# State reads of a retention layer: two batches at a time, on two 32-column strips of the array

## The reference, cut to what matters

```python
def retention_chunk(state, q, k, v, log_g):
    ...
    scores = jnp.einsum('bthd,bshd->bhts', q, k) * decay[None]
    inner = jnp.einsum('bhts,bshe->bthe', scores, v)
    q_decay = jnp.exp((i[:, None] + 1.0) * log_g[None, :])
    cross = jnp.einsum('bthd,bhde->bthe', q * q_decay[None, :, :, None], state)
    k_decay = jnp.exp((t - 1.0 - i)[:, None] * log_g[None, :])
    new_state = jnp.exp(t * log_g)[None, :, None, None] * state + jnp.einsum('bshd,bshe->bhde', k * k_decay[None, :, :, None], v)
    return new_state, inner + cross
```

## Time and profile before

| | |
|---|---|
| median of 3 runs | 3668.87 us (3668.02 to 3674.22) |
| span of the profiled execution | 3665.9 us |
| TensorE (PE) matmul busy, share of the span | 94% |
| VectorE (DVE), ScalarE (ACT), GpSimd (POOL) busy | 29%, 26%, 29% |
| DMA, mean over the span | 104 GB/s |
| mean granted TensorE clock | 0.977 of full |

### The profile page before, as it was taken

How to read it: one execution, slowest core, us unless ns; L and a number is a source line. 1 busy time by engine, 2 the same in 40 slices (tenths; PEclk the granted TensorE clock), 3 DMA queues, 4 the chain that set the end, 5 groups by cost and what they waited for, 6 DMA issues and landing times.

```text
span 3665.9 us, 43692 instructions
## 1 busy us (share of the span) xinstructions
PE 3442.4 (94%) x15505; PEld 2678.1 (73%) x15505; DVE 1048.2 (29%) x1920; ACT 947.2 (26%) x1465; POOL 1066.0 (29%) x444
## 2 busy tenths in 40 slices
PE   6799999999989889999999999999999989999877
PEld 5687777777877677686867767686867768778766
DVE  3401243232222341404132231404132240212234
ACT  4422333233223232121212212121212221222232
POOL 5542222232332023232322223232322223333211
PEclk9899999999999899999999999999999999999988
DMA  7333221223222233333333333333333444422231
GB/s 248 99 100 88 71 64 57 65 66 121 80 81 86 87 107 103 111 118 115 118 109 100 115 109 108 112 118 112 118 109 106 128 134 153 132 75 80 75 103 69
DMA packets 211747, 380.60 MB, mean 104 GB/s; under 512 B 20448, under 2 KB 59232, under 8 KB 207520
## 3 DMA queue, kind: packets, MB, share of 16 engines
q1 hardware_dynamic: 137744, 233.34, 20.6%
q10 hardware_dynamic: 73824, 144.84, 11.9%
HBM read 318.95 MB, written 60.16 MB: 103 GB/s over the span
## 4 chain that ended last, share of the span: by engine, by line
PE 72%; DVE 8%; issue 1%; ACT 1%; DVEq 1%; ACTq 0%
PE bank L544 17%; PE bank L546 16%; PE bank L545 16%; PE bank L548 4%; PE bank L549 4%; PE bank L855 2%; DVE R L1763 2%; PE bank L560 2%; PE bank L864 2%; PE bank L579 2%; DVE R L1761 1%; PE bank L903 1%; PE bank L899 1%; PE bank L825 1%; DVE stat L1501 1%
## 5 line engine op out<-in xcount | busy, mean ns | idle before, releaser
L521 POOL TENSOR_TENSOR w_lo<-w_raw,w_hi 128x1024 fp32r<-128x1024 f32 x440 | 1065.7, 2424 | 2554.8 <-ACT w_hi L961 2554.3
L544 PE MATMUL bank<-w_hi,xT_hi 128*128 128x512 f32 (+1 forms) x2880 | 1164.9, 404 | 20.5 <-DVE xT_sample L1526 8.9
L546 PE MATMUL bank<-w_hi,xT_lo 128*128 128x512 f32 (+1 forms) x2880 | 1123.4, 390 | 0.0
L545 PE MATMUL bank<-w_lo,xT_hi 128*128 128x512 f32 (+1 forms) x2880 | 1123.1, 390 | 0.0
L961 ACT ACTIVATE w_hi<-w_raw 128x1024 fp32r<-128x1024 f32 x440 | 466.2, 1061 | 1784.9 <-PE bank L549 1641.8
L544 PEld LDWEIGHTS bank<-w_hi,xT_hi 128*128 128x128 f32 x2880 | 545.5, 189 | 160.2 <-issue 29.8
L545 PEld LDWEIGHTS bank<-w_lo,xT_hi 128*128 128x128 f32 x2880 | 546.0, 190 | 115.8 <-issue 11.5
L546 PEld LDWEIGHTS bank<-w_hi,xT_lo 128*128 128x128 f32 x2880 | 544.8, 189 | 114.8
L548 PE MATMUL bank<-w_hi,xT_sample 128*128 128x512 f32 (+1 forms) x816 | 328.0, 402 | 5.2 <-DVE R L1761 5.2
L549 PE MATMUL bank<-w_lo,xT_sample 128*128 128x512 f32 (+1 forms) x816 | 316.8, 389 | 0.0
L973 ACT ACTIVATE R<-bank 128x512 f32<-128x512 f32 (+5 forms) x304 | 158.4, 526 | 371.1 <-PE bank L560 266.7
(11 more groups left out here) (171 smaller groups left out, 2485.6 us busy)
## 6 DMA issues: line engine op xcount, KB each, us to landing
w_raw<-in_w_in_ret SPq DMA_DIRECT2D x128, 512.0 KB, 3.7
w_raw<-in_w_in_even SPq DMA_DIRECT2D x80, 512.0 KB, 3.6
w_raw<-in_w_in_ret SPq DMA_DIRECT2D x128, 256.0 KB, 2.9
R<-in_state_ret ACTq DMA_DIRECT2D x64, 512.0 KB, 4.7
out_ret_state_sample<-R ACTq DMA_DIRECT2D x64, 512.0 KB, 3.1
w_raw<-in_w_out_ret SPq DMA_DIRECT2D x64, 512.0 KB, 3.6
w_raw<-in_w_out_even SPq DMA_DIRECT2D x32, 512.0 KB, 3.6
mix_scratch<-R ACTq DMA_DIRECT2D x16, 576.0 KB, 3.8
```

Source lines behind the costliest of these rows:

```text
L521: pool.tensor_tensor(wlo[:, s], raw[:, s], whi[:, s].bitcast(F32), ALU.subtract).then_inc(lo_ready, 1)
L544: pe.matmul(acc, th[:, k, tok], hi[:, kk, 0:width], start=first, stop=False)
L545: pe.matmul(acc, th[:, k, tok], lo[:, kk, 0:width], start=False, stop=False)
L546: mm = pe.matmul(acc, tl[:, k, tok], hi[:, kk, 0:width], start=False, stop=last)
```

## The change

The state reads of two batches are issued together. The batches are taken in the order `ORD` = 0, 4, 1, 5, 2, 6, 3, 7, for loads, stores, masked keys and reads alike. At even steps b the pair (b, b + 1) of that order is read: one of the batches 0 to 3, whose rows are 0 to 31 of the output, and one of the batches 4 to 7, whose rows are 32 to 63. `qz` holds 32 columns per batch in place of 64. Both states of a pair are waited for, each wait on an instruction of its own; then for each k there are two matmuls with a stationary operand of 128 x 32, one writing partitions 0 to 31 of bank 5, the other 32 to 63. At odd steps there is no state read; the state updates stay where they were.

```diff
+ORD = [b for g in range(DEC_B // 2) for b in (g, g + DEC_B // 2)]
+HB = NS // 2
...
-        qz, zm, rdec = c.take(2, DEC_B, NS), c.take(DEC_B, NS), c.take(P + NS)
+        qz, zm, rdec = c.take(2, DEC_B, HB), c.take(DEC_B, NS), c.take(P + NS)
...
-                    if m == 0:
-
-                        pe.wait_ge(state_in[b % 4], 32 * h + (16 * (b // 4) + 16))
+                    if m == 0 and b % 2 == 0:
+
+                        for n in (b, b + 1):
+                            pe.wait_ge(state_in[n % 4], 32 * h + (16 * (n // 4) + 16))
+                            wait_apart()
                         for k in range(2):
-                            mm = pe.matmul(bank[5][0:NS, :], qz[:, k, b], Wst[:, b % 4, k], start=False, stop=(b == 7 and k == 1))
-                        if b == 7:
+                            for n in (b, b + 1):
+                                half = slice(HB * (ORD[n] // 4), HB * (ORD[n] // 4) + HB)
+                                mm = pe.matmul(bank[5][half, :], qz[:, k, ORD[n]], Wst[:, n % 4, k], start=False, stop=(b == 6 and k == 1))
+                        if b == 6:
                             mm.then_inc(FULL(stage, "OI"), 1)
...
-                src = I.state_ret[0].rearrange("b h (k p) e -> b h p k e", p=P)[b, h]
+                src = I.state_ret[0].rearrange("b h (k p) e -> b h p k e", p=P)[ORD[b], h]
...
-                    dst = O.ret_state_sample[0].rearrange("b h (k p) e -> b h p k e", p=P)[b, h]
+                    dst = O.ret_state_sample[0].rearrange("b h (k p) e -> b h p k e", p=P)[ORD[b], h]
...
                     for k in range(2):
-                        ins = v.tensor_tensor(qz[:, k], qkT[:, k, SEQ:SEQ + NS].unsqueeze(1).to_broadcast([P, DEC_B, NS]), zm, ALU.mult)
+                        for g in range(2):
+                            q = qkT[:, k, SEQ + HB * g:SEQ + HB * (g + 1)].unsqueeze(1).to_broadcast([P, DEC_B // 2, HB])
+                            ins = v.tensor_tensor(qz[:, k, 4 * g:4 * g + 4], q, zm[:, 0:4, 0:HB], ALU.mult)
...
-                keys, col = QK[:, NT, RK:2 * RK], kz[:, bass.ds(DEC_B * h + b, 1)]
+                keys, col = QK[:, NT, RK:2 * RK], kz[:, bass.ds(DEC_B * h + ORD[b], 1)]
```

## The result

The changed kernel takes 3685.7 us (median of five runs, 3684.8 to 3687.3); the kernel before, beside it, 3670.9 (3668.0 to 3675.7). The ratio is 1.0042 [1.0029, 1.0055]: slower by some 15 us. The forecast was 3684.3. The state reads keep PE busy for 62 us less and the kernel is slower all the same.

The account below looks back on a forecast made before the run. PE was taken to bound the kernel, with 72% of the chain. The span of 3665.9 us, less 10.2 won, plus 25.6 for the clock, gave 3681.3; 3.0 up to the median made 3684.3, range 3659 to 3698 (8 in 10).

Parts of the forecast that it names:

- Even steps, 0 us more: State reads of a pair: eight 32-column passes run as four rounds of two, taking one batch's time now.
- Rivals 3 and 4: Pair reads: 32-column strips don't overlap, 3739 us, 6%; or strips start in strict program order, five rounds, 3698 us, 4%.
- Odd steps, 10.2 us won: State reads removed: 0.76 us won at batch 1, 0.52 at batch 7, none at 3 and 5, over eight heads.
- The waits of 1.3, 3, 4.4 and 1.5 us: Sign of being right: line 864 waits for the DVE's drain this long at the four odd batches.
- the prediction's paragraph on the clock: PE's idle times at batches 3 and 5 grow from 1.06 and 2.41 to 2.9 and 4.3 us, lowering the clock.
- Separate waits, state loads, masking, 0 us: Rest of the edit: 64 added sequencer waits, earlier waits for second state loads and four short masking multiplies cost nothing.
- Falls behind nearly all of the sixteen long waits: Granted clock drops after nearly all waits of batches 3 and 5 in eight heads, two now: 25.6 us net.
- rival 1: About half of the long waits, say those of batch 5, lose the clock: 3670 us, 15%.
- rival 2: Clock holds through the waits of batches 3 and 5, falls stay near two: 3658.7 us, 13%.
- The price, 1.8 us a fall: Mean loss per clock fall, taken from eight lone idle stretches of PE elsewhere in the trace.
- the sum: Profiled execution: 3665.9 - 10.2 + 25.6 = 3681.3 us, with 3.0 us carried from span to median: 3684.3.
- the prediction's 62%: Chance given to the forecast that most long waits lose the clock, with its own range of 3676 to 3692 us.

Follow-up runs that it names:

- experiment 7: Changed kernel with both batches of a pair on the same 64 partitions, 64 columns each, in order 0 to 7: 3731.3 us, ratio 1.0164.
- experiment 3: Changed kernel with six passes of zeros in PE's wait at step 3 and ten at step 5: 3657.2 us, ratio 0.9965.
- experiment 1: Kernel before with the odd steps' state reads left out, no strips or pairs, output lacking four batches: 3687.2 us, ratio 1.0048.
- experiment 4: Changed kernel with ten passes of zeros in the wait of step 5 alone, step 3 left idle: 3668.2 us, ratio 0.9988.
- Experiment 2: Changed kernel with four passes of zeros put into each wait at steps 3 and 5: 3663.0 us, ratio 0.9979.
- experiment 5: Changed kernel with the DVE's group norms of blocks 0 to 2 taken six positions after the output instead of three: 3587.5 us, ratio 0.9772.

## Why the prediction was right

- **Even steps, 0 us more.** Right: 1.91 us for eight passes (four rounds of 0.43, as against 2.3 for five and 3.65 measured in a row in experiment 7). Rivals 3 and 4 fall with it. In the trace the eight passes start in four pairs, 6 or 7 ns within a pair and 0.43 us from pair to pair. The program issues two passes of one strip, then two of the other, and passes on the same partitions follow each other (experiment 7); so the second of a pair is the other strip's, started ahead of a pass that was issued before it. The Trainium skill's rule of a strict program order (page "TensorE: Matmul & The Clock Gate", section "Part 3: Packing small matmuls — row/col tiling") would have given five rounds; the measurement decides against it here.
- **Odd steps, 10.2 us won.** 10.3 by experiment 3. The waits of 1.3, 3, 4.4 and 1.5 us that were to appear measure 1.0 (step 1), 2.9, 4.3 and 1.3 us by the timeline of the second head. All are a little below what was told, the long ones by 0.1, the short ones by 0.2 to 0.3; the 2.9 and 4.3 that the prediction's paragraph on the clock took from the rows are exact.
- **Separate waits, state loads, masking, 0 us.** Nothing contradicts it: no wait of PE for a state load appears, and experiment 1, which has none of the changed masking or loads, has the same time within 1.5 us.
- **Falls behind nearly all of the sixteen long waits.** 15 of 16, and rival 1 (half) and rival 2 (few) fall. Experiments 1, 3 and 4 show the cause: with the same waits and no strips the falls are there, with the waits filled they are gone, and with those of step 5 filled so are the falls behind step 5 and 17 of the 30 us.
- **The price, 1.8 us a fall.** Slightly too small: 2.0. The mean of lone idle stretches elsewhere counted mostly stretches with a mean clock of 0.70; behind step 5 it was 0.50 to 0.57 in all eight heads, 25 matmuls becoming 13 to 15, so 10 to 12 x 0.23 = 2.3 to 2.8 us; experiment 4, with two deeper falls of its own at step 3, leaves 17 / 8 = 2.1. One fall less and a higher price gave 30.0 - 3.2 = 26.8 in place of 25.6.

So the sum by measured terms is -10.3 + 26.8 = 16.5, which is the difference of the heads by construction; predicted were 15.4. That the time came out within 1.4 us is in part luck. On the spans the forecast was 3681.3 and the measurement 3685.5, 4.2 more: 1.1 in the heads, and 3.1 outside them, for which the sum had no term and no run shows a cause. Against this, the forecast added 3.0 us from span to median, and the median of the changed kernel lies 0.2 above its profiled span.

What the prediction could not have told is what experiment 7 shows: the same idle times with other surroundings cost some 14 us less. Experiment 2 says the same: five falls behind waits of 2.4 us, where the kernel before had two. The count of falls, and with it the size of the loss, was less certain than the prediction's 62% on nearly all of them made it look.

What the prediction didn't look for is the better version. It read that the DVE chain ahead of step 3's drain isn't shortened by the change, but not that the norm in this chain is needed only later.

## What to carry to other kernels

Before you take work off the busiest engine, look at what the next instruction waits for: where that doesn't come sooner by the change, work taken out just ahead of the wait gains nothing. Here it gained less than nothing on TensorE, because the clock fell after 15 of the 16 longer waits. Remove the wait first (here by an order in which the operation that is waited for precedes one that isn't urgent), then the work: the same change went from +15 to -52 us. And when an operation is moved back, ask who is waiting for what it now stands in front of.

## What the runs showed of the hardware

- **Idle TensorE work has a use.** 128 matmul instructions on zeros, in waits, shortened the kernel by 28.6 us (experiment 3).
- **A short VectorE operation can wait for GpSimd.** In the chain ahead of step 3's drain a multiply on one column takes ten times its usual time, here in the changed kernel (DVE, then POOL):

```profile
1699.75 1.68 DVE L1507 TENSOR_TENSOR stat<-stat 128x1 f32<-128x1 f32 x1
```

```profile
1699.03 2.38 POOL L523 TENSOR_TENSOR w_lo<-w_raw,w_hi 128x1024 fp32r<-128x1024 f32 x1 [9.32 <-ACT w_hi L967]
```

Both end at 1701.4. Ahead of step 5's drain it is the same, and both end near 1727.2:

```profile
1725.08 2.09 DVE L1507 TENSOR_TENSOR stat<-stat 128x1 f32<-128x1 f32 x1
```

```profile
1724.79 2.36 POOL L523 TENSOR_TENSOR w_lo<-w_raw,w_hi 128x1024 fp32r<-128x1024 f32 x1 [10.47 <-ACT w_hi L967]
```

In the eight heads of the changed kernel the 24 of these multiplies that start during this POOL operation take 0.29 to 2.1 us and end less than 0.02 us after it; the other 15 take 0.15 to 0.16. In experiment 5 the multiply of the norm from step 3 comes before the next POOL operation, which starts at 1694.08, and takes 0.16 us:

```profile
1693.32 0.16 DVE L1507 TENSOR_TENSOR stat<-stat 128x1 f32<-128x1 f32 x1
```

The 1.5 us between them would be half of step 3's wait. The Trainium skill, page "SBUF — State Buffer", section "Who interferes with whom", says that VectorE and GpSimd share a port pair, which one of them holds exclusively; the trace agrees, with 1.68 against 0.16 us. No experiment moved the POOL operation alone, so what the wait would lose by it isn't shown.
